# Segment sums from stored running sums, and the old states' decay inside VectorE's addition, in a hybrid decoder layer

## The reference, cut to what matters

```python
def ssd_chunked(x, dt, A, B, C, h0):              # 32 heads in 4 groups, chunks of 128 tokens
    ...
    a_cum = jnp.cumsum(jnp.moveaxis(a, 2, -1), axis=-1)             # a = dt * A
    tril = jnp.tril(jnp.ones((Q, Q), dtype=bool))
    seg = jnp.where(tril, a_cum[..., :, None] - a_cum[..., None, :], -jnp.inf)
    Lmat = jnp.exp(seg)
    CB = jnp.einsum('bclgn,bcsgn->bcgls', Cc, Bc)
    y_diag = jnp.einsum('bcgls,bcgels,bcsgep->bclgep', CB, Lmat, xdt)
    decay_to_end = jnp.exp(a_cum[..., -1:] - a_cum)
    chunk_states = jnp.einsum('bclgn,bcgel,bclgep->bcgepn', Bc, decay_to_end, xdt)
    chunk_decay = jnp.exp(a_cum[..., -1])
    def step(h, inp):
        dec, st = inp
        return h * dec[..., None, None] + st, h
    ...
    y_off = jnp.einsum('bclgn,bcgepn,bcgel->bclgep', Cc, h_prev, jnp.exp(a_cum))
```

## Time and profile before

| what | value |
|---|---|
| three runs | 1576.37, 1589.89, 1597.06 us; median 1589.89 |
| profiled execution | 1577.5 us, span 1576.0 us, granted clock 0.964 of 2.4 GHz |
| PE busy | 1470.1 us, 93% |
| DVE busy | 858.2 us, 54% |
| ACT busy | 627.6 us, 40% |
| POOL busy | 307.2 us, 19% |

### The profile page before, as it was taken

The page is one execution under the profiler, slowest core; times in us unless marked ns, Lnnn a source line. Parts: engine busy times, 40 slices in busy tenths (PEclk is TensorE's granted clock), DMA queues, the critical chain, the costliest instruction groups (busy, mean ns, idle before and its releaser), DMA issues. The chain is left out here.

```text
span 1576.0 us, 27390 instructions
## 1 busy us (share of the span) xinstructions
PE 1470.1 (93%) x10795; PEld 1380.9 (88%) x10795; DVE 858.2 (54%) x1076; ACT 627.6 (40%) x1029; POOL 307.2 (19%) x406
## 2 busy tenths in 40 slices
PE   5998999887899999899989999987999999999997
PEld 4997778776799898798988988877999999999997
DVE  3454547888326766766767566547444444442221
ACT  4574446776124433533532354133442323322211
POOL 2011231000021543343234405421200000000001
PEclk9999999998899998999999999888999999999999
DMA  3234663112242232232222322236222322222331
GB/s 110 81 94 150 196 214 91 45 50 71 70 143 68 81 97 65 64 92 81 75 81 81 94 74 81 81 86 215 70 80 81 91 81 80 80 86 89 100 101 46
DMA packets 190262, 146.29 MB, mean 93 GB/s; under 512 B 8392, under 2 KB 178544, under 8 KB 190111
## 3 DMA queue, kind: packets, MB, share of 16 engines
q1 hardware_dynamic: 175394, 97.93, 21.4%
q0 software_dynamic: 14384, 46.62, 9.5%
q10 hardware_dynamic: 384, 0.37, 0.1%
HBM read 124.51 MB, written 20.39 MB: 92 GB/s over the span
## 5 line engine op out<-in xcount | busy, mean ns | idle before, releaser
L431 PE MATMUL tile_banks<-x_hi,w_hi 128*128 128x288 f32 (+1 forms) x1808 | 521.3, 303 | 13.4 <-ACT gate_out L1592 7.6
L432 PE MATMUL tile_banks<-x_lo,w_hi 128*128 128x288 f32 (+1 forms) x1808 | 509.0, 297 | 0.0
L435 PE MATMUL tile_banks<-x_hi,w_lo 128*128 128x288 f32 (+1 forms) x1808 | 388.3, 296 | 0.0
L431 PEld LDWEIGHTS tile_banks<-x_hi,w_hi 128*128 128x128 f32 (+1 forms) x1808 | 343.3, 190 | 19.7 <-issue 10.0
L432 PEld LDWEIGHTS tile_banks<-x_lo,w_hi 128*128 128x128 f32 (+1 forms) x1808 | 342.9, 190 | 1.6
L405 DVE TENSOR_TENSOR w_lo<-w_raw,w_hi 128x1024 fp32r<-128x1024 f32 (+2 forms) x169 | 220.9, 1307 | 177.2 <-ACT w_hi L399 176.4
L435 PEld LDWEIGHTS tile_banks<-x_hi,w_lo 128*128 128x128 f32 (+1 forms) x1808 | 292.5, 189 | 0.4
L399 ACT ACTIVATE w_hi<-w_raw 128x1024 fp32r<-128x1024 f32 (+2 forms) x169 | 175.6, 1039 | 101.2 <-PE tile_banks L435 100.9
L432 PE MATMUL tile_banks<-f_lo,w_hi 128*128 128x288 f32 x352 | 98.2, 295 | 0.0
L431 PE MATMUL tile_banks<-f_hi,w_hi 128*128 128x288 f32 x352 | 97.8, 294 | 0.0
L888 POOL DMA_DIRECT2D out_y_prompt<-y_tok x8 | 6.3, 787 | 410.8 <-ACT y_tok L1859 399.1
(11 more groups left out here) (342 smaller groups left out, 2633.9 us busy)
## 6 DMA issues: line engine op xcount, KB each, us to landing
w_raw<-in_w_in SPq DMA_DIRECT2D x68, 512.0 KB, 3.7
w_raw<-in_w_gate SPq DMA_DIRECT2D x22, 512.0 KB, 3.7
w_raw<-in_w_up SPq DMA_DIRECT2D x22, 512.0 KB, 3.7
k_page<-in_cache_k SPq DMA_DIRECT2D x64, 128.0 KB, 2.7
v_page<-in_cache_v POOLq DMA_DIRECT2D x64, 128.0 KB, 2.9
old<-in_state_ssm POOLq DMA_DIRECT2D x32, 256.0 KB, 3.4
out_ssm_sample<-old POOLq DMA_DIRECT2D x32, 256.0 KB, 2.7
w_raw<-in_w_pb SPq DMA_DIRECT2D x16, 512.0 KB, 3.4
```

The costliest lines, as they stand in the source:

```text
L431: nc.tensor.matmul(out, wh, xh[:, HALVES[h]], start=start and k == 0, stop=False, skip_group_check=onto)
L432: nc.tensor.matmul(out, wh, xl[:, HALVES[h]], start=False, stop=False, skip_group_check=onto)
L435: mm = nc.tensor.matmul(out, wl, xh[:, HALVES[h]], start=False, stop=stop and k == last, skip_group_check=onto)
```

## The change

Four edits. (1) Segments: after the products that make decays, PE makes running sums of a over each chunk, with both signs, for all 32 heads as rows (5 small products), ACT and DVE store them as high and low parts in `sums` (128 rows: +hi, +lo, -hi, -lo by head). POOL stores the positive rows in DRAM on the diagonal of a matrix that was cleared before, so that reading it back gives for each group and chunk blocks of 8 heads by 8 x 128 with the head's row in its own column block only; this is `sum_rows`, 256 KB for each step, read two steps ahead into two buffers, and the other half of its rows are ones in diagonal form. ACT makes `picks` once a group: `sums` with all rows but the group's set to zero. One product of `picks` and `sum_rows` is then the running sum at l less that at s, and a second product of the bf16 mask `past` with `big_diag` adds a large negative number where s > l. `e` takes two products instead of four. `a_upto_hi`, `a_upto_lo`, `after_r` and `one_half` are gone. (2) The old states' decay is inside DVE's addition, four instructions for each sequence since the decay is a scalar by partition. (3) `xend` and `state` have one buffer instead of two. (4) The semaphores of key and value pages count four pages together.

```diff
-        keys += [("decays", 0)]
+        keys += [("decays", 0), ("sums", 0), ("sums", 1)]
...
+        def sums_diagonal(block):
+            return sums_dram[block].rearrange("a (h w) -> a h w", w=ROW)[:, :, 0:P]
+        def sums_matrix(block):
+            return sums_dram[block, :, 0:HG * HG * P].rearrange("a (h n) -> a h n", h=HG)
...
-                    eng.dma_start(k_page[:, n % K_SLOTS, :], cache_k[0, bass.ds(page_of(eng, x, k), 1)].rearrange("o p h d -> p (o h d)")).then_inc(sem(f"k_page_in{n % K_SLOTS}"), 16)
+                    eng.dma_start(k_page[:, n % K_SLOTS, :], cache_k[0, bass.ds(page_of(eng, x, k), 1)].rearrange("o p h d -> p (o h d)")).then_inc(sem(f"k_page_in{n // PART % (K_SLOTS // PART)}"), 16)
...
+            for n in range(6):
+                eng.dma_start(sums_matrix(n), zeros[:, :].unsqueeze(1).to_broadcast([2 * NH, HG, P])).then_inc(sem("sums_cleared"), 16)
+            eng.wait_ge(sem("sums_cleared"), 16 * 6)
+            eng.dma_start(sums_diagonal(5), ones[0:2 * NH, :].bitcast(F32R)).then_inc(sem("sums_cleared"), 16)
             for n in range(2):
                 gate_back(n)
...
-            def decay_steps(st):
+            def sums_in(st):
                 g, c = st // 5, st % 5
-                m, mask = (P, upto) if c < NC else (TS, upto_b)
-                if st:
-                    wait_full(eng, ("e" if (st - 1) % 5 else "seg", (st - 1) // 5, (st - 1) % 5, *(() if (st - 1) % 5 else (1,))))
-                for part, (src, dst) in enumerate(((a_hi, a_upto_hi), (a_lo, a_upto_lo))):
-                    eng.tensor_tensor(dst[0:m, :, 0:m], mask[0:m, 0:m].unsqueeze(1).to_broadcast([m, HG, m]),
-                                      f32(src[0:m, c, g * HG:(g + 1) * HG]).unsqueeze(2).to_broadcast([m, HG, m]),
-                                      ALU.mult).then_inc(sem("a_upto_made"), 1)
-                    eng.wait_ge(sem("a_upto_made"), 2 * st + part + 1)
-            eng.wait_ge(sem("a_split"), 2)
-            decay_steps(0)
-            for key in group_inputs(0):
+                if st >= 2:
+                    wait_full(eng, last_sums(st - 2))
+                eng.dma_start(sum_rows[0:2 * NH, st % 2], sums_matrix(c)).then_inc(sem(f"sums_in{st % 2}"), 16)
+            eng.wait_ge(sem("sums_cleared"), 16 * 7)
+            for n in range(2):
+                eng.dma_start(sum_rows[2 * NH:4 * NH, n], sums_matrix(5)).then_inc(sem(f"sums_in{n}"), 16)
+            eng.wait_ge(sem("sums_split"), 4)
+            for c, t0, m in token_tiles():
+                eng.dma_start(sums_diagonal(c)[:, :, 0:m], sums[0:2 * NH, t0:t0 + m]).then_inc(sem("sums_out"), 16)
+            conv_io(group_inputs(0)[0])
+            eng.wait_ge(sem("sums_out"), 16 * 5)
+            for st in range(2):
+                sums_in(st)
+            for key in group_inputs(0)[1:]:
                 conv_io(key)
             for g in range(NG):
...
-                    if g * 5 + c + 1 < STEPS:
-                        decay_steps(g * 5 + c + 1)
+                    if g * 5 + c + 2 < STEPS:
+                        sums_in(g * 5 + c + 2)
                     for key in before:
                         if key[0] in ("bc", "x"):
                             conv_io(key)
-                    if c < NC:
-                        for b in (2 * c, 2 * c + 1):
-                            wait_full(eng, ("old_t", g, b))
-                            eng.tensor_tensor(old[:, b % 2], old[:, b % 2],
-                                              seq_decay[:, g * PG:(g + 1) * PG, b:b + 1].to_broadcast([P, PG, P]), ALU.mult)\
-                               .then_inc(sem("old_decayed"), 1)
-                            eng.wait_ge(sem("old_decayed"), g * NB + b + 1)
                     for key in later:
                         if key[0] in ("bc", "x"):
                             conv_io(key)
...
+            pe.wait_ge(sem("a_signed_made"), 4)
+            for c, t0, m in token_tiles():
+                key = ("sums", c // NC)
+                mm = pe.matmul(spare(key)[:, t0 % TP:t0 % TP + m], a_signed[0:m, c].rearrange("p k h -> p (k h)"), (upto if c < NC else upto_b)[0:m, 0:m],
+                               start=c % NC == 0, stop=True, skip_group_check=True)
+                if c >= NC - 1:
+                    mm.then_inc(bank_full[use[key][0]], 1)
...
-                parts = [a[0:m, :, 0:m] for a in (a_upto_hi, a_upto_lo)]
-                pe.wait_ge(sem("a_upto_made"), 2 * (g * 5 + c + 1))
+                m, t0 = (P, c * P) if c < NC else (TS, TP)
+                st = g * 5 + c
+                mask = past if c < NC else past_b
+                rows = sum_rows[:, st % 2, :, 0:m]
+                pe.wait_ge(sem("picks_made"), g + 1)
+                pe.wait_ge(sem(f"sums_in{st % 2}"), 16 * (st // 2 + 2))
                 for q in range(2):
                     key = ("seg", g, c, q)
                     wait_read(pe, key)
                     out = spare(key)[0:m, :].rearrange("p (h l) -> p h l", l=P)[:, :, 0:m]
-                    for n, a in enumerate(parts):
-                        mm = pe.matmul(out, mask[0:m, 0:m], a[:, 4 * q:4 * q + 4, :], start=n == 0, stop=n == 1, skip_group_check=True)
-                    mm.then_inc(bank_full[use[key][0]], 1)
+                    pe.matmul(out, picks[:, t0:t0 + m], rows[:, 4 * q:4 * q + 4, :], start=True, stop=True, skip_group_check=True)
+                    pe.matmul(out, big_diag[0:m, 0:m], mask[0:m, 0:m].unsqueeze(1).to_broadcast([m, 4, m]), start=False, stop=True,
+                              skip_group_check=True).then_inc(bank_full[use[key][0]], 1)
                 if c:
                     key = ("e", g, c)
                     wait_read(pe, key)
                     out = spare(key).rearrange("p (j l) -> p j l", l=P)[:, :, 0:m]
                     for e in range(2):
-                        for n, a in enumerate(parts):
-                            mm = pe.matmul(out, one_half[0:m, e, :], a.rearrange("p (j e) l -> p j e l", e=2)[:, :, e, :],
-                                           start=e == 0 and n == 0, stop=e == 1 and n == 1, skip_group_check=True)
+                        mm = pe.matmul(out, picks[0:2 * NH, T + e * P:T + (e + 1) * P], rows[0:2 * NH].rearrange("p (j e) l -> p j e l", e=2)[:, :, e, :],
+                                       start=e == 0, stop=e == 1, skip_group_check=True)
...
+                eng.activation(picks[:, 0:T], f32(sums[:, :]), ACT.Copy, scale=group_rows[:, g:g + 1])
+                for e in range(2):
+                    at = T + e * P + e * HD
+                    ins = eng.activation(picks[0:2 * NH, at:at + HD], ones[0:2 * NH, 0:HD], ACT.Copy, scale=group_rows[0:2 * NH, g:g + 1])
+                ins.then_inc(sem("picks_made"), 1)
...
-                eng.wait_ge(sem("old_decayed"), n + 1)
-                eng.tensor_tensor(old[:, b % 2], old[:, b % 2], spare(key).rearrange("p (j n) -> p j n", j=PG), ALU.add)\
-                   .then_inc(bank_read[use[key][0]], 1)
+                for j in range(PG):
+                    ins = eng.scalar_tensor_tensor(out=old[:, b % 2, j, :], in0=old[:, b % 2, j, :], scalar=seq_decay[:, g * PG + j, b:b + 1],
+                                                   in1=spare(key)[:, j * P:(j + 1) * P], op0=ALU.mult, op1=ALU.add)
+                ins.then_inc(bank_read[use[key][0]], 1)
```

More of the change, by code:

```diff
@@ L1653, in _ @@
                 eng.wait_ge(sem(f"gated_out{e}"), 16 * (KD // 2))
[L1654 to L1658 removed]
             for rows, cs in ((slice(0, P), slice(0, NC)), (slice(0, TS), slice(NC, NC + 1))):
[L1660 removed]
+                n, m = cs.stop - cs.start, rows.stop
+                for k, sign in ((0, 1.0), (2, -1.0)):
+                    eng.activation(a_signed[rows, cs, k:k + 2, :], dt_tok[rows, cs, NH:2 * NH].unsqueeze(2).to_broadcast([m, n, 2, NH]), ACT.Copy,
+                                   scale=sign).then_inc(sem("a_signed_made"), 1)
             key = ("decays", 0)
@@ L1670, in _ @@
                .then_inc(bank_read[use[key][0]], 1)
+            for n, (cols, m) in enumerate(((slice(0, TP), TP), (slice(TP, T), TS))):
+                wait_full(eng, ("sums", n))
+                eng.activation(sums[:, cols], spare(("sums", n))[:, 0:m], ACT.Copy).then_inc(sem("sums_hi_made"), 1)
             def conv_silu(key):
```

99 lines of the change are left out of this document (60 added, 39 removed).

## The result

The changed kernel takes 1596.38 us (median of 20 runs, 1588.95 to 1610.85), the kernel before 1588.88 us beside it. The ratio is 1.0048, with an interval of 1.0028 to 1.0069: some 7.5 us slower, where 18 us faster was forecast. The profiled execution took 1594.4 us, near its median, while that of the kernel before (1577.5) was at the fast end of its runs (1576.37 to 1602.89). A second profile of the kernel before, among the experiments, is the fairer partner.

The account below looks back on a forecast made before the run. PE was taken as the bound, busy 1470.1 of 1576.0 us. Segments -7.0, contention stalls -12.4 and opening +1.1 gave -18.3 us; taken off 1583.7 that forecast 1565.4 us, range 1547 to 1586.

Parts of the forecast that it names:

- The segments' saving: State-space steps on PE: e products halved from four to two in 16 steps, 9.9 us less 2.9 lost to waits, -7.0 us.
- The clock: PE's granted clock, 512 to 1050 us: no term in the sum, treated only as rival C.
- rival C: State-space stretch: fewer clock dips give about -13 us more, 1552, or a dip elsewhere costs +5; chance 0.20.
- The contention: Group starts: a_upto leaves POOL, DVE's xend comes sooner, four PE stalls of about 3.1 us go, -12.4 us.
- The opening: Before the state-space steps: five f32 running-sum products on PE, 0.26 us each for the four larger, +1.1 us.
- DVE's additions: Old states' decay: four DVE instructions, 1.37 us, +0.68 a sequence, covered by 2 us of idle time, 0 on PE.
- Pages and buffers: Merged page semaphores and one buffer for xend and state: PE waits for a page once, 0.3 us; 0.
- The part after 1050 us: Merge and feed-forward part: taken as untouched by the change, no term in the sum.
- A: Group starts: stalls go only in part, xend_s stays long behind POOL's b_seq and DMA issues; -12.7, 1571 us; chance 0.17.
- D: State-space steps: savings fall into later stalls, the change gives nothing, 1581 to 1587 us; chance 0.12.
- B: State-space sequences: DVE's fourfold addition delays PE by 0.68 us in each of 32, together +3.5, 1587 us; chance 0.06.
- the signs listed as wrong: Changed profile: PE waiting for sum_rows or picks, xend over 2 us, additions well over 1.4, new e_t/decay/w_lo waits over 5.

Follow-up runs that it names:

- e9: Kernel before, with the four e products of each 128-token step using only the first 64 rows, same number of products and columns; ratio 1.016 to before.
- e4: Kernel before, with POOL making a_upto for the first step only and PE multiplying stale buffers in the other 19; ratio 0.9824 to before.
- e10: Kernel before, with one added wait: POOL starts a step's masks only when DVE has made xend; ratio 0.9864 to before.
- e1: Kernel before, with only the old states' decay moved from POOL into DVE's addition as four instructions; ratio 1.0004 to before.
- e11: e3 with a semaphore for each key page again, value pages' still merged; ratio 0.9944 to the kernel before.
- e8: Kernel before, unchanged, run again for a second profiled execution; 1588.9 us.
- e3: Changed kernel, with the 128-token steps' mask product in fp32r and the e products over all 128 rows, zeros added; ratio 0.991 to before.
- e12: e3 run again unchanged, with a second profile; ratio 0.9953 to the kernel before.
- e6: Changed kernel, with only the e products over 128 rows, mask still bf16; ratio 0.9992 to the kernel before.
- e5: Changed kernel, with only the 128-token steps' mask product in fp32r, e still over 64 rows; ratio 1.0058 to the kernel before.

## Why the prediction was wrong

**The segments' saving (-7.0).** This is the step that failed. I counted products and columns: two fewer of 512 columns, half of 19.8 us. The `e` products had also gone from 128 rows to 64, which stands in the diff (`picks[0:2 * NH]`) and which I didn't price at all; the bf16 mask I did, at 0. Measured: 0.04 us a step at the full clock instead of 0.45, about 0.2 instead of 0.85 at half, and in the 64-token steps a loss: the four take 7.7 us in all where they took 6.8. So four steps are +1.0, the twelve others about -1 to -1.5, and -7.0 was about 0.

**The clock (0 in the sum).** I had it give in rival C, and take 5 at most. Against the second profile of the kernel before it took 52.9 - 41.0 = 11.9 us, and that is as much as the stalls gave. e9 shows that 64-row products do this without any other edit.

**The contention (-12.4).** Right, and to the size: 14.9 - 2.0 = 12.9 us of waits for `xend` went. (One reading was off and changes nothing: 40 `a_upto` instructions left POOL, not 32; a pair for each of 20 steps, of which 4 cover 64 tokens.) e4 and e10 show that by itself this is worth more than its waits, 22 to 28 us.

**The opening (+1.1).** Too small: the running sums' products take 2.62 us.

```profile
466.06 0.69 PE L1183 MATMUL spare_bank<-e_t,ones 64*64 64x128 f32 x4 [2.56 <-POOL e_t L828]
466.68 2.07 PE L1190 MATMUL spare_bank<-upto,decay 128*128 128x128 f32 x8
468.68 0.69 PE L1190 MATMUL spare_bank<-upto_b,decay 64*128 64x64 f32 x2
469.30 0.61 PE L444 MATMUL tile_banks<-x_hi,w_hi 128*128 128x288 f32 x1
```

Ten instructions, eight of them at 0.25 each: PE comes out of a 2.56 us wait at half clock. I took the price from products at the full clock for a place behind a wait.

**DVE's additions (0 on the path).** Right, by e1 and by their 343 ns. DVE fell to 815.7, well under the 848 to 860 forecast, since the contention had also stretched `y_t` L2204, the state's product and `w_lo`. POOL is 213.2 for "about 200". Neither shows at the end.

**Pages and buffers (0).** PE's waits for key pages rose to 4.1, and by e11 nothing shows that they reach the end.

**The part after 1050 us (0).** I had it untouched. The same 1091 PE instructions of the feed-forward's last part, from the first one of `f_hi` to the last transposes of `prod`, first in e8, then in the changed kernel:

```profile
1434.93 0.30 PE L431 MATMUL tile_banks<-f_hi,w_hi 128*128 128x288 f32 x1
...
1577.97 0.55 PE L1378 MATMUL spare_bank<-ident,prod 128*128 128x128 f32 x3 [0.85 <-DVE prod L2338]
```

```profile
1437.43 0.30 PE L444 MATMUL tile_banks<-f_hi,w_hi 128*128 128x288 f32 x1
...
1582.80 0.66 PE L1410 MATMUL spare_bank<-ident,prod 128*128 128x128 f32 x4 [0.85 <-DVE prod L2395]
```

That is 143.0 us against 145.4, at the full clock in both. All eight profiles with the new segments, those of e3 and e12 too, have 145.4; the six without them have 142.5 to 143.0. The merge (first `x_again` to `root`) adds another 0.5. So some 3 us go to something that the new program does to unchanged work; what it is, no run shows.

**The sum again**, against e8's profile: clock +11.9, stalls -12.9, opening +2.6, 64-token steps +1.0, the other segments about -1, the part after 1050 us +3, which makes about +5; the spans differ by 1592.7 - 1587.4 = 5.3 and the medians by 7.5. That the sum closes so well is in part luck, since two executions of the same kernel differ by more (11 us here). Of the miss of 31 us (1596.4 for 1565.4) 5 are the base: I took the sum off 1583.7, and the median of before is 1588.9.

The rivals of the prediction: A and D are out, since the stalls went whole and no wait took their place. B came nearest in the time and was the wrong mechanism; the slower side came from PE's own products. The range ended at 1586, ten short, and even B's own 1587 lay outside of it. None of the signs listed as wrong appeared, for none was a sign of PE's own products; the one that failed was PE's busy time, 23.6 us up instead of 9 down.

## What to carry to other kernels

A product that is added or replaced is counted by its rows and type too, not by its columns alone: put zeros in and keep the shape of its neighbours (more rows to multiply gained 9 us on the changed kernel in e6, and with the mask's type 15 to 22 in e3 and e12). Look for the price in the old trace first: the 64-token steps had it. When the profile shows one engine's instruction stretched by another's, first try to move the other (e10: one wait, 22 us) before rebuilding what it computes. And where a kernel's profiled execution lies at the edge of its runs, take a second profile before the sum is made against it, and compare the clock over all runs.

## What was not expected of the hardware

- Products over 64 of 128 rows between ones over 128 cost 0.1 us on each of two products at each border, where no weight load runs ahead, and lower the granted clock of the stretch: 0.90 instead of 0.93 (e9), 0.89 and 0.91 instead of 0.93 (e5 and the changed kernel against e3 and e6). Over all runs it is 0.944 against 0.958 for e9. Whether it is the fewer rows or the short holdups at the borders that bring the clock down was not separated; holdups from a change of type alone (e6) came with 0.956, between the changed kernel's 0.952 and e3's 0.961.
- Two profiled executions of the kernel before took 1577.5 and 1588.9 us with the same stalls for `xend` (14.8 and 14.9 us); 6.9 of the 11 us between them are the clock in the state-space stretch.
- The new additions of DVE, with one tensor in SBUF and one in PSUM, never run beside a computing instruction of POOL, neither in the changed kernel nor in e1, so their 339 to 349 ns say nothing of contention. The kernel before has an instruction that does: `e_t<-e_t,spare_bank` (L2202) runs 12 times at 128x512, each time beside a TENSOR_TENSOR of POOL, and takes 686 to 689 ns, against 688 in the changed kernel. Its neighbour `y_t<-y_t,e_t` (L2204), with both in SBUF, takes 1191 ns on average against 692. The Trainium skill, in "SBUF — State Buffer", section "Who interferes with whom", says that an instruction of VectorE with at most one SBUF input, outside its 2-port modes, does not contend with GpSimd; the trace agrees.
- The same 1091 PE instructions at the full clock take 2.4 us more in every kernel with the new segments, 400 us behind the last of them (145.4 against 143.0). The cause is open.
